# NSA layer of a four-layer hybrid trunk: queries projected ahead of the keys, compressed softmax in two halves, first scores ahead of the last projection

## The chip, the cores and the metric

One core of one Trainium2 chip. The metric is device time in microseconds (us) of one execution, lower is better; three runs give a median. The core has TensorE (PE, matrix products, with its weight loads shown apart as PEld), VectorE (DVE), ScalarE (ACT), GpSimd (POOL) and SyncE (SP, which here only starts DMA loads). Each engine works through its own queue in order, and semaphores tie the queues together.

## The reference, cut to what matters

A trunk of two layers on 256 tokens of width 1024. Each layer is FFN, token mixer, FFN, each wrapped in RMS norms with a residual. The first layer's mixer is native sparse attention (NSA), the second's is a softmax attention with a forget gate (FoX). Only the NSA mixer is touched:

```
q, kc, vc, ks, vs, kw, vw, gates = split(h @ w_in)       # 16 query heads of 64, 4 key groups
k_cmp = gelu(blocks(kc) @ w1[0] + b1[0]) @ w2[0]         # 15 blocks of 32 tokens, stride 16
v_cmp = gelu(blocks(vc) @ w1[1] + b1[1]) @ w2[1]
p_c   = masked_softmax(q @ k_cmp.T * scale + bias_c)     # compressed branch, 15 columns a head
o     = g0 * (p_c @ v_cmp) + g1 * attend(q, ks, vs) + g2 * attend(q, kw, vw)
return o @ w_out
```

With 256 tokens the selected branch sees all causal keys, as the window branch does, so both are full causal attentions.

## The kernel before, in words

Weights come in units of 1 MB (128 partitions by 2048 floats) in a ring of three slots. For each unit SP loads `raw`; ACT makes the rounded part `whi` (`hi`, L446), DVE the rest `wlo` (`lo`, L651), and PE multiplies in three products, which gives nearly fp32 precision. `hi` of unit u waits until PE is through with unit u - 3, so the splitting runs beside the products.

The NSA sub-layer has ten projection units, k = 0 to 9, of 256 columns each, then four units of output rows. PE takes the units in order; ACT copies each result from PSUM (`evacuate(k)`, L594, signal `proj_ready`). The column list in the SP queue sets the order: values of both branches (k = 0, 1), compressed keys and values (2, 3), selected keys (4), window keys (5), then the queries in four units (6 to 9), all 16 heads in eight pairs.

Between the projections the compressed branch is prepared. POOL shifts tokens by DMA (`pair_tokens`) into `pairs`; DVE gathers them and adds the position term into `flat` (`gather`, L818); PE runs `compress_hidden(kv)` (32 instructions), ACT copies (`part_out`, L598), PE folds (`compress_fold`), ACT takes GELU (L603), PE makes `compress_out(kv)`. Before, PE does hidden(0) behind k = 5, fold(0) behind 6, out(0) behind 7, hidden(1) behind 8, fold(1) behind 9. DVE's `gather(0)` stands in its queue behind `lo` of unit 7, two steps after the gate's reciprocal (L827). POOL also copies keys to the other half of the partitions by DMA (`kX`).

Then `attend` runs 16 stages n (head pair n // 2, branch n % 2) as a written-out order with a lag of three. In step i PE does `scores(i)`, something out of the table `after_scores`, `probs_T(i - 3)` (six transposes, L1186) and `heads(i - 4)`; DVE does `logits(i)` (L747), something out of `after_logits`, the copy of the transposes (L769) and `factors(i - 1)` (L756, L760); ACT does the exponentials of stage i (L542); POOL scales them (L372). PE's `probs_T(n)` waits for DVE's copy of stage n - 1. The compressed scores of all heads (32 products), their maximum, subtraction, exponential, sum and scaling (DVE L881 to L904, ACT L627), the values (L908) and eight transposes (L1282) with their two copies (L913) sit in steps 0, 1 and 2 of these tables, all behind the last projection.

Of the kernel before, what the change touches and what calls it, by code (L numbers as in the profile page):

```python
# [106 lines left out]
def trunk(nc, x, norm_g, w_gate, w_up, w_down, rel_bias, nsa_in, cmp_pe, cmp_w1, cmp_b1, cmp_w2,  # L107
          nsa_out, fox_in, fox_bf, fox_out, consts, onehots, out, scratch):
    with ExitStack() as ctx:
# [112 lines left out]
        kx_in = sem("kx_in")  # L222
# [43 lines left out]
        def _(sp):  # L266
# [33 lines left out]
            for s, kind in enumerate(KINDS):  # L300
# [17 lines left out]
                else:  # L318
                    w, wo = (nsa_in[0], nsa_out[0]) if kind == "nsa" else (fox_in[0], fox_out[0])
                    cols = [1792, 2304, 1024, 1280, 1536, 2048, 0, 256, 512, 768] if kind == "nsa" else [UC * k for k in (8, 9, 10, 11, 0, 1, 2, 3, 4, 5, 6, 7)]  # L320
# [13 lines left out]
        def _(pool):  # L334
# [72 lines left out]
            for r in range(2):  # L407
                pool.wait_ge(proj_ready, 5 + r)
                for a in range(2):
                    pool.dma_start(kX[64 * (1 - a):64 * (1 - a) + 64, r, :, :], kN[64 * a:64 * a + 64, r, :, :]).then_inc(kx_in, 16)  # L410
# [7 lines left out]
            nc.gpsimd.memset(pairs[:, :], 0.0).then_inc(probc_zero, 1)  # L418
            for n in range(H):
                scale_probs(n)  # L420
# [19 lines left out]
        def _(act):  # L440
# [91 lines left out]
            def attend(kind, out_unit):  # L532
# [16 lines left out]
                for i in range(N + LAG + 2):  # L549
                    if i >= LAG + 2 and (i - LAG - 1) % per == 0:  # L550
                        heads_hi((i - LAG - 1) // per - 1)
                    if i < N:
                        exps(n0 + i)
                    if i in (N, N + 2):
                        hi_static(out_unit + (i - N) // 2)
# [12 lines left out]
            for s, kind in enumerate(KINDS):  # L568
# [3 lines left out]
                else:  # L572
                    nproj = 10 if kind == "nsa" else 12

                    def evacuate(k):
# [4 lines left out]
                        if kind == "nsa":  # L580
                            if k >= 6:
                                dst, scale = qT[:, 2 * (k - 6):2 * (k - 6) + 2, :], DH ** -0.5
                            else:
                                dst = [vN[:, 0], vN[:, 1], kcv[:, 0], kcv[:, 1], kN[:, 0], kN[:, 1]][k]
# [14 lines left out]

                    def gelu(kv):  # L600
                        act.wait_ge(hid_mm, kv + 1)
                        for m in range(2):
                            last = nc.scalar.activation(hid[:, m, :], ps[:, MB, HID + m * 64:HID + m * 64 + G * NC], ACT.Gelu_apprx_tanh,  # L603
                                                        bias=smallT[:, 32 + 2 * kv + m:33 + 2 * kv + m])
                        last.then_inc(hid_ready, 1)
                    hi_static(u0 + 2)
                    for k in range(1, nproj):
                        evacuate(k - 1)
                        hi_static(u0 + k + 2)
# [3 lines left out]
                        if kind == "nsa" and k in (6, 9):  # L613
                            part_out((k - 6) // 3)
                        if kind == "nsa" and k == 7:
                            gelu(0)
                        if kind == "fox" and k == 3:
# [10 lines left out]
                    attend(kind, u0 + nproj + 2)  # L628
# [19 lines left out]
        def _(dve):  # L648
# [152 lines left out]
            for s, kind in enumerate(KINDS):  # L801
# [3 lines left out]
                else:  # L805
                    nproj = 10 if kind == "nsa" else 12

                    def gather(kv):
# [9 lines left out]
                        nc.vector.tensor_tensor(dst, src, pe_, ALU.add).then_inc(flat_ready, 1)  # L818
                    lo_static(u0 + 2)
                    for k in range(1, nproj):  # L820
                        lo_static(u0 + k + 2)
                        if kind == "nsa":
# [5 lines left out]
                            if k == 5:  # L828
# [4 lines left out]
                            if k == 8:  # L833
# [33 lines left out]
                    if kind == "nsa":  # L867
                        dve.wait_ge(hid_ready, 2)
                        dve.wait_ge(hidR_zero, 1)
                        for m in range(2):  # L870
                            src = hid[:, m, :]
                            src = bass.AP(src.tensor, src.offset, [list(src.ap[0]), [NC, G], [0, 4], [1, NC]])
                            last = nc.vector.tensor_copy(hidR[:, m, :, :, 0:NC], src)
                        last.then_inc(hidR_ready, 1)

                        dve.wait_ge(sc_mm, 1)
                        s3 = sc[:, :, :, :].rearrange("p t h c -> p (t h) c")

                        c1 = (P - CB) // CS + 1
                        s_ = ps[:, OB, 0:TT * H * NC].rearrange("p (t h c) -> p t h c", t=TT, c=NC)  # L880
                        nc.vector.tensor_tensor(sc[:, 0, :, 0:c1], s_[:, 0, :, 0:c1], bias[:, :, P + CB - 1:S:CS], ALU.add)  # L881
                        nc.vector.tensor_scalar(sc[:, 0, :, c1:NC], s_[:, 0, :, c1:NC], NEG, None, ALU.add)
                        nc.vector.tensor_tensor(sc[:, 1, :, :], s_[:, 1], bias[:, :, CB - 1:S:CS], ALU.add).then_inc(sc_step, 1)
                        dve.wait_ge(sc_step, 1)
                        nc.vector.tensor_reduce(cmx[:, :, :].rearrange("p t h -> p (t h)"), s3, AX.X, ALU.max).then_inc(sc_step, 1)
                        dve.wait_ge(sc_step, 2)
                        def spread(v):
                            return bass.AP(v[:, :, :].tensor, v[:, :, :].offset, [list(v[:, :, :].ap[0]), [1, TT * H], [0, NC]])
                        nc.vector.tensor_tensor(s3, s3, spread(cmx), ALU.subtract).then_inc(sc_logits, 1)

                    def compressed_probs():
                        dve.wait_ge(sc_exp, 1)
                        nc.vector.tensor_reduce(csum[:, :, :].rearrange("p t h -> p (t h)"), s3, AX.X, ALU.add).then_inc(sc_step, 1)
                        dve.wait_ge(sc_step, 3)
                        nc.vector.reciprocal(cfac[:, :, :], csum[:, :, :]).then_inc(sc_step, 1)
                        dve.wait_ge(sc_step, 4)

                        for t in range(TT):
                            last = nc.vector.scalar_tensor_tensor(cfac[:, t, :], cfac[:, t, :], cst[:, C_VALID + t:C_VALID + t + 1],
                                                                  gate[:, t, 0:H], ALU.mult, ALU.mult)  # L900
                        last.then_inc(sc_step, 1)
                        dve.wait_ge(sc_step, 5)
                        dve.wait_ge(probc_zero, 1)
                        nc.vector.tensor_tensor(probc.rearrange("p t h c -> p (t h) c")[:, :, 0:NC], s3, spread(cfac), ALU.mult).then_inc(probc_ready, 1)  # L904

                    def compressed_values():
                        dve.wait_ge(cmp_mm, 2)
                        nc.vector.tensor_copy(vcmp[:, :, :], ps[:, MB, 0:256].rearrange("p (g d) -> p g d", g=G)).then_inc(cmp_ready, 1)  # L908

                    def compressed_transposed():  # L910
                        for t in range(TT):
                            dve.wait_ge(probcT_mm, t + 1)
                            nc.vector.tensor_copy(probcT[:, :, t * P:(t + 1) * P],  # L913
                                                  ps[:, MB - t, :].rearrange("p (g n) -> p g n", g=G)).then_inc(probcT_ready, 1)
                    attend(kind, u0 + nproj + 2, {0: compressed_probs, 1: compressed_values, 2: compressed_transposed} if kind == "nsa" else {})
# [25 lines left out]
        def _(pe):  # L941
# [202 lines left out]
            def attend(kind, after_scores, out_rows, projected):  # L1144
# [22 lines left out]
                def scores(n):  # L1167
                    b = n % 2
                    if n >= 2:
# [9 lines left out]
                def probs_T(n):  # L1179
                    b = n % PB  # L1180
                    pe.wait_ge(prob_ready, n + 1)
                    if n >= 1:
                        pe.wait_ge(probT_ready, n)
                    for a in range(2):
# [4 lines left out]
                def heads(n):  # L1189
# [13 lines left out]
                    if compressed:  # L1203
                        if n == n0:
                            pe.wait_ge(probcT_ready, 2)
# [7 lines left out]
                for i in range(N + LAG + 1):  # L1213
# [10 lines left out]
                    if LAG <= i < N + LAG:  # L1224
                        probs_T(n0 + i - LAG)
# [6 lines left out]
            for s, kind in enumerate(KINDS):  # L1232
# [7 lines left out]
                for k in range(nproj):  # L1240
                    if k >= 2:
                        pe.wait_ge(proj_ready, pr0 + k - 1)
                        by_token = kind == "fox" and k < 4
                        (tokens if by_token else features)(u0 + k, (u0 + k) % RING, GB + k % 2)
                    if kind == "nsa" and k == 2:
                        gates(OB, 0, 48)
                    if kind == "nsa" and k == 5:
                        pe.wait_ge(gate_ready, 1)
                        for t in range(TT):
                            last = nc.tensor.transpose(ps[:, OB, S + 48 * t:S + 48 * (t + 1)], gateT[:, t * P:(t + 1) * P], cst[0:48, C_ID:C_ID + 48])  # L1250
# [69 lines left out]
```

## Time and the profile before

| what | value |
|---|---|
| median of 3 runs | 1083.14 us (1082.77 to 1083.49) |
| the profiled execution's own time | 1083.23 us |
| its span, first to last instruction | 1081.4 us |
| instructions | 18063 |
| PE busy | 1050.9 us, 97% of the span |
| DVE busy | 574.4 us, 53% |
| ACT busy | 483.0 us, 45% |
| mean granted PE clock | 0.993 of full |

The page gives busy times as shares of the span; a busy share is a mean over stretches with different limits. The NSA sub-layer lies between some 215 and 370 us of the span. Time of an execution stands 1.83 us over its span (launch and end).

### The profile page before, as it was taken

Reading aid. Unit: us, or ns where it says so; the run is one execution under the profiler, and the core shown is the slowest. Engines: PE = TensorE matmul, PEld = TensorE weight load, DVE = VectorE, ACT = ScalarE, POOL = GpSimd, SP = SyncE. Lnnn points to the kernel's source line nnn. Section 1 sums busy time; section 2 is a strip of 40 time slices with the busy share of each in tenths; the row PEclk is TensorE's granted clock in tenths of the full one; section 3 lists DMA queues with packets and bytes.
Section 4 is the critical chain, followed back from the end, with each engine's and each line's share of the span. In section 5 each row is a group of like instructions: output and inputs, shape, how many; then the busy total and the mean of one; then the engine's idle time right before and its main releaser. Section 6 shows DMA issues by size and latency. Waiting matters only on the chain.

```text
span 1081.4 us, 18063 instructions
## 1 busy us (share of the span) xinstructions
PE 1050.9 (97%) x7489; PEld 962.5 (89%) x7489; DVE 574.4 (53%) x645; ACT 483.0 (45%) x615; POOL 104.5 (10%) x207
## 2 busy tenths in 40 slices
PE   6999999999989999999999999999999999999997
PEld 6897999999856799999989999999999779999996
DVE  4543454554487555444566445445555765454444
ACT  4434434454375354444354434444456635434432
POOL 0100000122054200000011000000123420000000
PEclk8999999999989999999999999999999999999999
DMA  9686555477401275655646565555555136556551
GB/s 278 213 304 224 167 192 194 156 221 248 135 2 40 82 244 180 194 187 166 197 150 225 171 196 187 194 183 167 196 156 194 41 97 226 168 190 194 172 178 39
DMA packets 137813, 187.80 MB, mean 174 GB/s; under 512 B 7249, under 2 KB 120102, under 8 KB 137766
## 3 DMA queue, kind: packets, MB, share of 16 engines
q1 hardware_dynamic: 133702, 172.90, 49.8%
q0 software_dynamic: 3920, 14.18, 3.8%
q8 instruction: 34, 0.56, 0.2%
q14 instruction: 13, 0.11, 0.0%
q10 hardware_dynamic: 144, 0.07, 0.0%
HBM read 184.48 MB, written 1.07 MB: 172 GB/s over the span
## 4 chain that ended last, share of the span: by engine, by line
PE 89%; DVE 4%; ACT 2%; issue 2%; POOL 2%; SPq 1%; DMA 1%; DVEq 0%; ACTq 0%
PE ps L943 86%; PE ps L1186 2%; DVE normed L683 1%; POOL ms_half L343 1%; DVE normed L663 1%; ACT ps L466 1%; DMA raw<-in_ffn_w_gate 1%; ACT whi L446 1%; POOL rstd L349 1%; PE ps L1023 1%; DVE xlo L691 0%; DVE probT_buf L769 0%; DVE res L672 0%; SPq L291 0%; SPq L282 0%
## 5 line engine op out<-in xcount | busy, mean ns | idle before, releaser
L651 DVE TENSOR_TENSOR wlo<-raw,whi 128x2048 fp32r<-128x2048 f32 x156 | 358.0, 2295 | 320.1 <-ACT whi L446 320.1
L943 PE MATMUL ps<-xhi,whi 128*128 128x256 f32 x1536 | 435.8, 284 | 0.0
L943 PE MATMUL ps<-xlo,whi 128*128 128x256 f32 x1536 | 434.6, 283 | 0.0
L943 PE MATMUL ps<-xhi,wlo 128*128 128x256 f32 x1536 | 434.6, 283 | 0.0
L446 ACT ACTIVATE whi<-raw 128x2048 fp32r<-128x2048 f32 x156 | 297.5, 1907 | 112.7 <-PE ps L943 110.7
L943 PEld LDWEIGHTS ps<-xhi,whi 128*128 128x128 f32 x1536 | 294.6, 192 | 3.4 <-issue 2.0
L943 PEld LDWEIGHTS ps<-xlo,whi 128*128 128x128 f32 x1536 | 294.7, 192 | 1.6 <-issue 0.2
L943 PEld LDWEIGHTS ps<-xhi,wlo 128*128 128x128 f32 x1536 | 294.7, 192 | 0.0
L943 PE MATMUL ps<-whi,hhi 128*128 128x512 f32 x320 | 125.0, 391 | 0.0
L943 PE MATMUL ps<-wlo,hhi 128*128 128x512 f32 x320 | 125.0, 391 | 0.0
L943 PE MATMUL ps<-whi,hlo 128*128 128x512 f32 x320 | 124.5, 389 | 0.0
L943 PE MATMUL ps<-whi,xhi 128*128 128x256 f32 (+1 forms) x320 | 104.5, 326 | 8.7 <-DVE xlo L691 8.7
L943 PE MATMUL ps<-wlo,xhi 128*128 128x256 f32 (+1 forms) x320 | 101.8, 318 | 0.0
L943 PE MATMUL ps<-whi,xlo 128*128 128x256 f32 (+1 forms) x320 | 101.7, 318 | 0.0
L493 ACT ACTIVATE hhi<-work 128x512 fp32r<-128x512 f32 x36 | 22.7, 631 | 164.3 <-DVE work L698 164.3
L943 PEld LDWEIGHTS ps<-whi,xhi 128*128 128x128 f32 x320 | 62.0, 194 | 14.9 <-issue 7.9
L347 POOL TENSOR_SCALAR ms<-ss 128x1 f32<-128x1 f32 x14 | 4.8, 341 | 718.3 <-ACT ps L470 718.3
L943 PEld LDWEIGHTS ps<-whi,hlo 128*128 128x128 f32 x320 | 60.1, 188 | 12.8
L943 PEld LDWEIGHTS ps<-whi,hhi 128*128 128x128 f32 x320 | 60.2, 188 | 11.5
L943 PEld LDWEIGHTS ps<-wlo,hhi 128*128 128x128 f32 x320 | 60.2, 188 | 11.0
L484 ACT ACTIVATE work<-ps 128x512 f32<-128x512 f32 x44 | 26.3, 598 | 91.6 <-PE ps L943 91.5
L943 PEld LDWEIGHTS ps<-whi,xlo 128*128 128x128 f32 x320 | 62.0, 194 | 3.9
(171 smaller groups left out, 832.0 us busy)
## 6 DMA issues: line engine op xcount, KB each, us to landing
raw<-in_ffn_w_gate SPq DMA_DIRECT2D x44, 1024.0 KB, 5.3
raw<-in_ffn_w_up SPq DMA_DIRECT2D x44, 1024.0 KB, 5.3
raw<-in_ffn_w_down SPq DMA_DIRECT2D x44, 1024.0 KB, 4.9
raw<-in_fox_w_in SPq DMA_DIRECT2D x12, 1024.0 KB, 5.4
raw<-in_nsa_w_in SPq DMA_DIRECT2D x10, 1024.0 KB, 5.3
big<-in_nsa_cmp_w POOLq DMA_DIRECT2D x2, 2048.0 KB, 11.3
raw<-in_nsa_w_out SPq DMA_DIRECT2D x4, 1024.0 KB, 5.0
raw<-in_fox_w_out SPq DMA_DIRECT2D x4, 1024.0 KB, 4.9
```

Of the source, the lines that this page charges most:

```text
L343: nc.gpsimd.tensor_scalar(ms_half[:, j:j + 1], ss_half[:, j:j + 1], scale / D, eps, ALU.mult, ALU.add).then_inc(half_mean, 1)
L349: nc.gpsimd.tensor_tensor(rstd[:, i:i + 1], ms[:, i:i + 1], half[:, :], ALU.pow).then_inc(rstd_ready, 1)
L446: nc.scalar.activation(whi[:, slot, :], raw[:, slot, :], ACT.Copy).then_inc(w_hi, 1)
L466: nc.scalar.activation(ps[:, OB, :], res[:, t, 0:512], ACT.Square, accum_out=ss_half[:, j:j + 1]).then_inc(half_sumsq, 1)
L484: nc.scalar.activation(silu_sb, ps[:, GB, :], ACT.Silu).then_inc(silu_ready, 1)
L493: nc.scalar.activation(dst[:, 0:2, :], src.rearrange("p (a n) -> p a n", a=2), ACT.Copy).then_inc(hhi_ready, 1)
L651: nc.vector.tensor_tensor(wlo[:, slot, :], raw[:, slot, :], whi[:, slot, :].bitcast(F32), ALU.subtract).then_inc(w_lo, 1)
L663: nc.vector.tensor_tensor(normed[:, t, :].rearrange("p (a n) -> p a n", a=2), ps[:, YB + 2 * t:YB + 2 * t + 2, :], g_post[:, :].rearrange( ...
L683: nc.vector.scalar_tensor_tensor(normed[:, t, cols], res[:, t, cols], rstd[:, i:i + 1], g_pre[:, cols], ALU.mult, ALU.mult).then_inc(norme ...
L943: return nc.tensor.matmul(out_, l, r, start=start, stop=stop)
L1023: last = nc.tensor.transpose(ps[:, GB + 2 * t + b, k * P:(k + 1) * P], normed[:, t, (4 * b + k) * P:(4 * b + k + 1) * P], ident)
L1186: last = nc.tensor.transpose(ps[:, GB + a, k * P:(k + 1) * P], prob[b][:, a, k * P:(k + 1) * P], ident)
```

## The change

- The projection order: the first two query units move ahead of the selected and window keys (columns 0 and 256 become k = 4 and 5, the keys k = 6 and 7).
- PE: `compress_hidden(0)` behind k = 4 and not 5, fold(0) behind 5, out(0) behind 6; `compressed_scores(0)`, for the first eight heads, and hidden(1) behind 7; fold(1) behind 8. `scores(0)` and `scores(1)` come ahead of projection 9, which is now in `attend` behind `scores(1)`. The second half of the compressed scores and out(1) follow `scores(2)`. The transposes are split in four (step 3), two (ahead of `probs_T(4)`) and two (ahead of `probs_T(5)`).
- DVE: `gather(0)` directly behind the gate's reciprocal (k = 4), `gather(1)` at 6, the keys' copy at 7, first softmax half at 8 and 9; in `attend` the second half: logits in step 2, maximum in 3, probabilities in 5; transposed copies in 3, 7 and 8; `lo` of unit 11 in step 1.
- ACT: exponential of the first half at k = 8, second GELU at 9, projection 9's copy behind the exponentials of stage 1, the second half's exponential behind those of stage 4.
- POOL: the `kX` copies go behind both `pair_tokens`, the load of the second `w1` and the clearing of `pairs`, with a semaphore for each branch.

```diff
-cols = [1792, 2304, 1024, 1280, 1536, 2048, 0, 256, 512, 768]
+cols = [1792, 2304, 1024, 1280, 0, 256, 1536, 2048, 512, 768]
@@ POOL: moved behind the memset of pairs
-for r in range(2):
-    pool.wait_ge(proj_ready, 5 + r)
+for r in range(2):
+    pool.wait_ge(proj_ready, 7 + r)
@@ ACT
+if kind == "nsa" and k == 9: gelu(1)          # behind evacuate(8)
+if k in (5, 8): part_out((k - 5) // 3)
+if k == 6: gelu(0)
+if k == 8: compressed_exp(0)
-    evacuate(nproj - 1)
-    gelu(1)
-    act.wait_ge(sc_logits, 1)
-    nc.scalar.activation(sc[:, :, :, :], sc[:, :, :, :], ACT.Exp).then_inc(sc_exp, 1)
+    attend(kind, u0 + nproj + 2, {1: lambda: evacuate(9), 4: lambda: compressed_exp(1)})
@@ DVE
-if k == 5:
+if k == 4:
     gather(0)
-if k == 7:
+if k == 6:
     gather(1)
+if k == 8:
+    compressed_logits(0)
+    compressed_max(0)
+if k == 9:
+    compressed_probs(0)
-attend(..., {0: compressed_probs, 1: compressed_values, 2: compressed_transposed})
+attend(..., {0: spread_hidden, 1: lambda: lo_static(u0 + 11), 2: second_compressed, 3: first_transposed,
+             5: lambda: compressed_probs(1), 7: lambda: later_transposed(2), 8: lambda: later_transposed(3)})
+def second_compressed():
+    compressed_logits(1)
+    dve.wait_ge(cmp_mm, 2)
+    nc.vector.tensor_copy(vcmp[:, :, :], ps[:, MB, 0:256]...).then_inc(cmp_ready, 1)
+def first_transposed():
+    compressed_max(1)
+    dve.wait_ge(probcT_mm, 1)
+    nc.vector.tensor_copy(probcT[:, 0:2, :], ps[:, MB, :]...).then_inc(probcT_ready, 1)
@@ PE
+for k in range(9):
+    if k >= 2: project(k)
+    if k == 4: compress_hidden(0)
+    if k == 5: (gate transposes); compress_fold(0)
+    if k == 6: compress_out(0)
+    if k == 7:
+        pe.wait_ge(gate_ready, 2)
+        pe.wait_ge(cmp_ready, 1)
+        compressed_scores(0)
+        compress_hidden(1)
+    if k == 8: compress_fold(1)
+attend(kind, {1: last_projection, 2: second_compressed, 3: first_T}, {7: lambda: later_T(2), 8: lambda: later_T(3)},
+       out_rows, (proj_ready, pr0 + nproj))
+def second_compressed():
+    pe.wait_ge(sc_step, 1)
+    pe.wait_ge(proj_ready, pr0 + 10)
+    compressed_scores(1)
+    compress_out(1)
+def first_T():
+    pe.wait_ge(probc_ready, 1)
+    pe.wait_ge(cmp_ready, 2)
+    # four transposes for groups 0 and 1
```

## Rows read from the trace of the kernel before

**Rows 1.** The page, busy time, share of the span and instructions of each engine.
```profile
PE 1050.9 (97%) x7489; PEld 962.5 (89%) x7489; DVE 574.4 (53%) x645; ACT 483.0 (45%) x615; POOL 104.5 (10%) x207
```
**Rows 2.** Waits of PE, 230 to 420 us: total, times, longest.
```profile
PE ps L1282 <- DVE vcmp L908: 2.7, 1, 2.7
...
PE ps L943 <- DVE xlo L691: 1.2, 1, 1.2
PE ps L943 <- DVE nmax L747: 0.8, 1, 0.8
...
PE ps L943 <- DVE flat L818: 0.5, 1, 0.5
```
**Rows 3.** Stretches of 4 us: engines' busy time, then clock, DMA share, GB/s.
```profile
core 0: us, PE busy (x) PEld busy (x) DVE busy (x) ACT busy (x) POOL busy (x), PEclk, DMA share, GB/s
...
296.00:300.00 4.00, 1.39 (x13) 0.85 (x11) 3.90 (x21) 2.47 (x9) 0.00 (x0) 0.83 0.00 0
300.00:304.00 4.00, 3.14 (x16) 2.50 (x16) 3.62 (x19) 3.58 (x16) 1.73 (x5) 0.50 0.02 4
304.00:308.00 4.00, 3.71 (x26) 2.50 (x24) 3.40 (x18) 1.89 (x9) 2.44 (x7) 0.82 0.01 2
...
372.00:376.00 4.00, 2.83 (x24) 2.62 (x23) 4.00 (x6) 2.19 (x6) 0.79 (x2) 1.00 0.00 0
```
**Rows 4.** PE in order of time: start, duration, what, idle before.
```profile
257.19 3.67 PE L943 MATMUL ps<-big,flat 128*64 128x256 f32 x32 [0.54 <-DVE flat L818]
...
289.92 3.76 PE L943 MATMUL ps<-kcmp,qT 128*128 128x30 f32 x32
...
300.86 1.94 PE L1282 MATMUL ps<-cst,pairs 128*128 128x128 f32 x8 [2.67 <-DVE vcmp L908]
...
306.87 0.85 PE L1186 MATMUL ps<-cst,work 128*128 128x128 f32 x6 [0.29 <-DVE probT_buf L769]
```
**Rows 5.** DVE in order of time, around the first gather.
```profile
247.35 2.29 DVE L651 TENSOR_TENSOR wlo<-raw,whi 128x2048 fp32r<-128x2048 f32 x1 [6.22 <-ACT whi L446]
...
249.88 1.75 DVE L827 RECIPROCAL work<-work 48x256 f32<-48x256 f32 x1
...
255.32 1.81 DVE L818 TENSOR_TENSOR flat<-pairs,smallT 128x960 f32<-128x960 f32 x1
```
**Rows 6.** ACT in order of time.
```profile
250.68 0.60 ACT L594 ACTIVATE kN<-ps 128x512 f32<-128x512 f32 x1 [3.37 <-PE ps L943]
251.17 1.90 ACT L446 ACTIVATE whi<-raw 128x2048 fp32r<-128x2048 f32 x1
256.44 0.60 ACT L594 ACTIVATE kN<-ps 128x512 f32<-128x512 f32 x1 [3.36 <-PE ps L943]
...
289.27 0.51 ACT L603 ACTIVATE hid<-ps,smallT 128x60 f32<-128x60 f32 x2
289.80 1.28 ACT L627 ACT_TABLE_LOAD   x1
...
297.24 0.40 ACT L542 ACTIVATE work<-work,nmax 128x128 f32<-128x128 f32 x1 [0.51 <-DVE nmax L747]
...
298.92 0.18 ACT L542 ACTIVATION_READ_ACCUMULATOR work<-work,nmax 128x1 f32 x1
```
**Rows 7.** DVE in order of time, in the opening of the attention.
```profile
296.02 0.28 DVE L747 CUSTOM_DVE_ANT_0 work<-ps,bias 128x128 f32<-128x128 f32 x1
...
297.13 0.65 DVE L893 TENSOR_REDUCE csum<-sc 128x32 f32<-128x480 f32 x1
...
298.61 0.66 DVE L904 TENSOR_TENSOR pairs<-sc,cfac 128x480 f32<-128x480 f32 x1
...
302.02 1.50 DVE L913 COPY flat<-ps 128x512 f32<-128x512 f32 x2
...
305.76 0.96 DVE L769 COPY probT_buf<-ps 128x768 f32<-128x768 f32 x1
```
**Rows 8.** The chain that ended last, two pieces in the steady attention.
```profile
310.75 1.66 PE ps L943 x16
312.41 0.81 PE ps L1186 x6
```

More of the change, by code:

```diff
@@ L418, in _ @@
             nc.gpsimd.memset(pairs[:, :], 0.0).then_inc(probc_zero, 1)
+            for r in range(2):
+                pool.wait_ge(proj_ready, 7 + r)
+                for a in range(2):
+                    pool.dma_start(kX[64 * (1 - a):64 * (1 - a) + 64, r, :, :], kN[64 * a:64 * a + 64, r, :, :]).then_inc(kx_in[r], 16)
             for n in range(H):
@@ L530, in ffn, with attend @@
                 hi_static(u0 + 33)
-            def attend(kind, out_unit):
+            def attend(kind, out_unit, after_exps):
                 n0, p0, N = STAGE0[kind], PAIR0[kind], STAGES[kind]
@@ L598, in part_out, with compressed_exp @@
                         nc.scalar.activation(hid_part, ps[:, MB, 0:HID], ACT.Copy).then_inc(part_ready, 1)
+                    def compressed_exp(r):
+                        act.wait_ge(sc_logits, r + 1)
+                        v = sc[:, :, 8 * r:8 * r + 8, :]
+                        nc.scalar.activation(v, v, ACT.Exp).then_inc(sc_exp, 1)
                     def gelu(kv):
@@ L608, in _ @@
                         evacuate(k - 1)
+                        if kind == "nsa" and k == 9:
+                            gelu(1)
                         hi_static(u0 + k + 2)
@@ L622, in _ @@
                             nc.scalar.activation(fT[:, 3, :], fT[:, 2, :], ACT.Ln, bias=1.0).then_inc(f_ln, 1)
-                    evacuate(nproj - 1)
                     if kind == "nsa":
-                        gelu(1)
-                        act.wait_ge(sc_logits, 1)
-                        nc.scalar.activation(sc[:, :, :, :], sc[:, :, :, :], ACT.Exp).then_inc(sc_exp, 1)
-                    attend(kind, u0 + nproj + 2)
+                        attend(kind, u0 + nproj + 2, {1: lambda: evacuate(9), 4: lambda: compressed_exp(1)})
+                    else:
+                        evacuate(nproj - 1)
+                        attend(kind, u0 + nproj + 2, {})
                     for k in range(2, 3):
@@ L818, in gather, with heads_part, spread, compressed_logits @@
                         nc.vector.tensor_tensor(dst, src, pe_, ALU.add).then_inc(flat_ready, 1)
+                    def heads_part(v, r):
+                        return v[:, :, 8 * r:8 * r + 8]
+                    def spread(v, r):
+                        v = heads_part(v, r)
+                        return bass.AP(v.tensor, v.offset, [list(d) for d in v.ap] + [[0, NC]])
+                    c1 = (P - CB) // CS + 1
+                    def compressed_logits(r):
+                        dve.wait_ge(sc_mm, r + 1)
+                        hs = slice(8 * r, 8 * r + 8)
+                        s_ = ps[:, OB, 0:TT * H * NC].rearrange("p (t h c) -> p t h c", t=TT, c=NC)
+                        nc.vector.tensor_tensor(sc[:, 0, hs, 0:c1], s_[:, 0, hs, 0:c1], bias[:, hs, P + CB - 1:S:CS], ALU.add)
+                        nc.vector.tensor_scalar(sc[:, 0, hs, c1:NC], s_[:, 0, hs, c1:NC], NEG, None, ALU.add)
+                        nc.vector.tensor_tensor(sc[:, 1, hs, :], s_[:, 1, hs, :], bias[:, hs, CB - 1:S:CS], ALU.add).then_inc(sc_step, 1)
@@ new lines, in compressed_max, with compressed_probs @@
+                    def compressed_max(r):
+                        s_ = heads_part(sc, r)
+                        dve.wait_ge(sc_step, 5 * r + 1)
+                        nc.vector.tensor_reduce(heads_part(cmx, r), s_, AX.X, ALU.max).then_inc(sc_step, 1)
+                        dve.wait_ge(sc_step, 5 * r + 2)
+                        nc.vector.tensor_tensor(s_, s_, spread(cmx, r), ALU.subtract).then_inc(sc_logits, 1)
+                    def compressed_probs(r):
+                        s_ = heads_part(sc, r)
+                        hs = slice(8 * r, 8 * r + 8)
+                        dve.wait_ge(sc_exp, r + 1)
+                        nc.vector.tensor_reduce(heads_part(csum, r), s_, AX.X, ALU.add).then_inc(sc_step, 1)
+                        dve.wait_ge(sc_step, 5 * r + 3)
+                        nc.vector.reciprocal(heads_part(cfac, r), heads_part(csum, r)).then_inc(sc_step, 1)
+                        dve.wait_ge(sc_step, 5 * r + 4)
+                        for t in range(TT):
+                            last = nc.vector.scalar_tensor_tensor(cfac[:, t, hs], cfac[:, t, hs], cst[:, C_VALID + t:C_VALID + t + 1],
+                                                                  gate[:, t, hs], ALU.mult, ALU.mult)
+                        last.then_inc(sc_step, 1)
+                        dve.wait_ge(sc_step, 5 * r + 5)
+                        dve.wait_ge(probc_zero, 1)
+                        nc.vector.tensor_tensor(heads_part(probc, r)[:, :, :, 0:NC], s_, spread(cfac, r), ALU.mult).then_inc(probc_ready, 1)
@@ new lines, in spread_hidden @@
+                    def spread_hidden():
+                        dve.wait_ge(hid_ready, 2)
+                        dve.wait_ge(hidR_zero, 1)
+                        for m in range(2):
+                            src = hid[:, m, :]
+                            src = bass.AP(src.tensor, src.offset, [list(src.ap[0]), [NC, G], [0, 4], [1, NC]])
+                            last = nc.vector.tensor_copy(hidR[:, m, :, :, 0:NC], src)
+                        last.then_inc(hidR_ready, 1)
+                    def second_compressed():
+                        compressed_logits(1)
+                        dve.wait_ge(cmp_mm, 2)
+                        nc.vector.tensor_copy(vcmp[:, :, :], ps[:, MB, 0:256].rearrange("p (g d) -> p g d", g=G)).then_inc(cmp_ready, 1)
@@ L867, in _ @@
                     if kind == "nsa":
[L868 to L876, printed above, removed]
@@ L891, in compressed_probs @@
[L891 to L904, printed above, removed]
@@ L906, in compressed_values @@
[L906 to L914, printed above, removed]
@@ L1142, in compress_out, with attend @@
                 last.then_inc(cmp_mm, 1)
-            def attend(kind, after_scores, out_rows, projected):
+            def attend(kind, after_scores, before_heads, out_rows, projected):
                 n0, p0, N = STAGE0[kind], PAIR0[kind], STAGES[kind]
@@ L1168, in scores @@
                     b = n % 2
+                    if kind == "nsa" and n < 2:
+                        pe.wait_ge(kx_in[n], 32)
                     if n >= 2:
@@ L1177, in scores, with probs_T @@
                     last.then_inc(scores_mm, 1)
-                def probs_T(n):
+                def probs_T(n, extra=None):
                     b = n % PB
@@ L1204, in heads @@
                         if n == n0:
-                            pe.wait_ge(probcT_ready, 2)
+                            pe.wait_ge(probcT_ready, 1)
+                            pe.wait_ge(sc_step, 6)
+                        elif n in (8, 12):
+                            pe.wait_ge(probcT_ready, n // 4)
                         for a in range(2):
@@ L1224, in attend @@
                     if LAG <= i < N + LAG:
-                        probs_T(n0 + i - LAG)
+                        probs_T(n0 + i - LAG, before_heads.get(i))
                     if i == N + LAG:
@@ L1239, in _ @@
                 nproj = 10 if kind == "nsa" else 12
[L1240 to L1250, printed above, removed]
-                        last.then_inc(gateT_mm, 1)
-                    if kind == "nsa" and k in (5, 8):
-                        compress_hidden((k - 5) // 3)
-                    if kind == "nsa" and k in (6, 9):
-                        compress_fold((k - 6) // 3)
-                    if kind == "nsa" and k == 7:
-                        compress_out(0)
-                    if kind == "fox" and k == 1:
-                        gates(MB, 48, GWC)
-                    if kind == "fox" and k == 5:
-                        pe.wait_ge(cum_ready, 1)
-                        mm(ps[:, MB, 0:S], cst[0:2 * H, C_SEL:C_SEL + P], cum[:, :], True, True).then_inc(cum_mm, 1)
@@ L1289, in heads_of, with project @@
+                def project(k):
+                    pe.wait_ge(proj_ready, pr0 + k - 1)
+                    by_token = kind == "fox" and k < 4
+                    (tokens if by_token else features)(u0 + k, (u0 + k) % RING, GB + k % 2)
                 def heads_of(k):
```

123 lines of the change are left out of this document (74 added, 49 removed).

## The prediction, made before the changed kernel ran

> **What bounds the kernel now.** I read the page first: PE is busy for 97% of the span [rows 1]. So a reordering pays only where PE stands still or runs at the lower clock, and costs wherever it makes PE stand. Next the waits of PE around the NSA sub-layer [rows 2]: 0.5 us for `flat`, 0.8 for the logits (L747), 2.7 for the compressed branch behind `vcmp`; PE's own order of time adds 0.3 before the second `probs_T` [rows 4]. Together 4.3 us. Then the granted clock [rows 3]: 0.83, 0.50 and 0.82 in three stretches of 4 us. With 0.5 as the low level (1.2 of 2.4 GHz), 1.36 us of the first and 1.44 of the last were low, so the clock fell at about 298.6 and rose at about 305.4. PE had been idle 0.80 us and then, after the short scores, was in an idle of 2.67. It worked from 300.86 [rows 4] to 305.4 at half clock, 4.6 us, which lost 2.3. What this opening costs in all is 4.3 + 2.3 = 6.6 us, and that is also the most that the change can give back here: every product is still done, and steady attention shows PE without a wait (the chain stays on PE there [rows 8]).
>
> **The change part by part.** I walk the new order with the old durations. Up to the end of projection 4, which is where `evacuate(4)` starts, 250.68 [rows 6], nothing is moved.
>
> *Wait A, the first gather.* `compress_hidden(0)` now stands directly behind projection 4 and needs `gather(0)`. The gather is one of DVE's items of step 4: `lo` of unit 6 starts at 247.35 because it waits for ACT, then comes the reciprocal from 249.88 for 1.75, to 251.63, then the gather, 1.81 [rows 5]. It ends at 253.4. PE is done at 250.6 and stands 2.8 us, with everything behind it in its queue. Before, a projection of 5.76 us (the distance of two `evacuate` starts [rows 6]) and the gate's transposes lay between, and 0.54 was left [rows 4]. The gather needs nothing later than the paired tokens, whose DMAs are long issued, so nothing but DVE's own queue sets this. `lo` of unit 7 is then behind the gather by about 0.4 us and is not wanted for another ten.
>
> *Projections 5 to 8.* With PE 2.3 us later than before, I checked each wait. The second `w1` is loaded behind hidden(0) and is wanted 20 us later. `pairs` is cleared and `kX` copied some 10 us ahead of `scores(0)`, though POOL's copies now wait behind both token shifts, the `w1` load and the clearing. The first softmax half on DVE and ACT (about 2.5 us with its table load of 1.28 [rows 6]) lies under projection 8. The `kcmp` copy ends about 1 us before PE asks; this is the thinnest cover, and what it misses comes straight to PE. SP's load of unit 14 waits for `lo` of unit 11, now in `attend`: some 10 us later, but wanted after all 16 stages. Cost nothing.
>
> *Wait B, the last evacuation.* After projection 8 PE has the fold (0.5), `scores(0)` and `scores(1)`, projection 9 (5.76) and `scores(2)`. A stage's scores take half of 1.66 [rows 8], 0.83. That makes 8.8. ACT in the same time has, in order, `evacuate(8)` 0.6, a table load 1.28, GELU 0.5, `hi` of unit 11 1.9, the table load back 1.28, the exponentials of stages 0 and 1, 1.87 each (297.24 to 299.10), and `evacuate(9)` 0.6 [rows 6]: 9.9. PE's second compressed scores wait for that copy: 9.9 - 8.8 = 1.1; I take 1.05 as some ACT instructions overlap by 0.1.
>
> *Wait C, step 4.* `probs_T(1)` waits for DVE's copy of stage 0. From the end of `scores(3)` DVE has `logits(3)` 1.11 (296.02 to 297.13 [rows 7]), the half maximum and subtraction, the copy of 512 columns 0.75 (half of 1.50) and the copy of stage 0, 0.95 [rows 7]. Half of a 480-column operation lies between half of 0.65 and all of it; half the columns suggest half plus the overhead of a small one, 0.37, so 0.74 for two. Sum 3.6. PE meanwhile does four transposes (0.55, as eight took 1.94 at half clock [rows 4]), `probs_T(0)` 0.81 [rows 8] and `scores(4)` 0.83: 2.2. PE stands 1.4.
>
> *Wait D, step 6.* The second half's probabilities sit ahead of the copy of stage 2. The whole took from 297.13 to 299.27, 2.1 [rows 7]; the half lies between 1.05 and 2.1, I take 1.4. DVE: 1.11 + 1.4 + 0.95 = 3.5; PE: `probs_T(2)` 0.81 and heads with scores 1.66 [rows 8]: 2.5. PE stands 1.0. After that DVE has the two late copies, some 0.4 each, and the next waits come out with 0.2 to 0.4 us to spare.
>
> The halving itself adds no product; the compressed scores are 16 + 16 for 32 [rows 4]. *Sum at full clock:* A 2.8 + B 1.05 + C 1.4 + D 1.0 = 6.3 against 6.6 removed: -0.3 us. The bounds: C and D each from 0.4 less to 0.9 more by the two ends for a half, B from 0 to 1.3; so from -2.1 to +1.8.
>
> *The clock.* The trace has no idle of 2.8 us inside dense projections, so its price is unknown: nothing at the least, and at the most 3.4, half of the 6.8 us that the low stretch lasted, if all of it were work. The nearest row is the fall at 298.6: it came in an idle of 2.67 us with 0.80 shortly before. An idle of 1.17 to 1.2 with dense work around it [rows 2] left the clock at 1.00 [rows 3]. A is far nearer the first. I take a fall, at the 2.3 us that the old one lost. Waits B and C come with light work between them, the 16 products of 30 columns among it, as in the old opening; a second fall there is a little likelier than not. It also costs 2.3 us, but DVE goes on at its pace, and about half of C and D (1.2) closes up: 1.1 net.
>
> The Trainium skill (TensorE: Matmul & The Clock Gate, "Why this matters for your kernels") says that the clock holds if no idle between bursts of matmuls passes about 3 us. The row of this trace speaks against it, for a gap of 2.67, but with 0.80 shortly before. By that rule wait A would leave the clock alone, and the sum would stay at -0.3; by the row it is 2.3 higher.
>
> **Total.** -0.3 + 2.3 + 1.1 = +3.1 us on the profiled 1083.23 gives 1086.3; the median of the runs stands 0.1 under that execution, so 1086.2.
>
> **The rivals.** 0.2% (2.2 us) is what a measurement of this kernel can tell from no change.
> - *One fall only* (after A, or in the opening): -0.3 + 2.3 = +2.0, 1085.1. For it: B and C are each shorter than the old idle. 28 in 100.
> - *The clock holds through all four waits*: -0.3, 1082.8. This is the skill's rule, as a mechanism: idles of at most 2.8 cost themselves alone. Against it stands the fall at 298.6 [rows 3]. 10 in 100.
> - *Faster: DVE keeps up in the opening*, so that B, C and D do not come, and the clock holds. Then -6.6 + 2.8 = -3.8, 1079.3. It decides when DVE's 3.6 us behind `scores(3)` come under PE's 2.2, and likewise in step 6; against it stand the durations [rows 7]. With a fall after A it would be -1.5, no measurable change. 8 in 100.
> - *Worse:* the falls last over more work, or C and D stay beside them: -0.3 + 3.4 + 2.3 = +5.4 at the end, 1088.5; middle 1087.8. 12 in 100.
> - *My forecast*, two falls: 42 in 100.
>
> **How the numbers follow.** Slower by over 2.2: nearly all of the forecast (0.38), nearly half of the one-fall case (0.13), all of the worse (0.12): 0.63. Faster: the faster rival and a touch of the bounds: 0.09. Within: the rest, 0.28. The range for 8 in 10 leaves out the faster rival and the far end of the worse: 1082.6 to 1088.3. For the forecast alone it is 1085.0 to 1087.4.
>
> **What would show it.** In the profile after: a wait of PE for `flat` of 2.8 us near 250.6, followed by stretches of clock under 1.00 in projection 5; the wait before L1282's old place gone; a wait for ACT's `qT` copy of about 1 us behind `scores(2)`; waits for `probT_buf` of 1.4 and 1.0; a second low stretch there; two table loads more on ACT; from stage 8 on the old pace. The prediction is wrong if the clock row shows 1.00 after `flat`, if the opening's waits are missing, or if a cover I counted as free (the `kcmp` copy, the `kX` copies) shows as a wait of PE.

## The result, and the profile after

The changed kernel takes 1086.24 us (median of 7 runs, 1084.33 to 1087.67) against 1083.06 us (7 runs, 1082.77 to 1083.49): 3.2 us more, ratio 1.0027 with a 95% interval of 1.0016 to 1.0038. It is slower by 0.27%, and a ratio of 1 lies outside the interval. The profiled execution took 1085.29 us with a span of 1083.5 us, 2.1 us over that of the kernel before; the median span over the seven executions is 1084.2 us. An execution's time stands between 1.8 and 3.3 us over its span in these seven, not always by the 1.83 us of the profile before.

The waits of PE around the NSA sub-layer, against [rows 2] (same columns):

```profile
PE ps L1229 <- DVE probT_buf L780: 3.0, 4, 1.2
PE ps L982 <- DVE flat L829: 2.6, 1, 2.6
PE ps L982 <- DVE xlo L702: 1.2, 1, 1.2
PE ps L982 <- ACT qT L597: 1.1, 1, 1.1
```

Of the kernel before, one line of the same view belongs beside these:

```profile
PE ps L1186 <- DVE probT_buf L769: 1.3, 3, 0.7
```

The waits for `vcmp` (2.7) and for the logits (0.8) are gone. In their place stand the gather (2.6, before 0.5), the copy of projection 9 (1.1, new), and the copies of the transposes (3.0 in four waits, before 1.3 in three). In PE's order of time, against [rows 4]:

```profile
252.92 5.36 PE L982 MATMUL ps<-big,flat 128*64 128x256 f32 x32 [2.65 <-DVE flat L829]
...
298.12 1.94 PE L982 MATMUL ps<-kcmp,qT 128*128 128x30 f32 x16 [1.12 <-ACT qT L597]
307.18 0.84 PE L1229 MATMUL ps<-cst,work 128*128 128x128 f32 x6 [0.79 <-DVE probT_buf L780]
313.97 0.85 PE L1229 MATMUL ps<-cst,normed 128*128 128x128 f32 x6 [1.24 <-DVE probT_buf L780]
```

These are waits A, B, C and D: 2.65, 1.12, 0.79 and 1.24, together 5.8 us where 4.3 stood before. The 32 instructions of `compress_hidden(0)` also took 5.36 us where they took 3.67. Stretches of 4 us show why, against [rows 3]:

```profile
core 0: us, PE busy (x) PEld busy (x) DVE busy (x) ACT busy (x) POOL busy (x), PEclk, DMA share, GB/s
252.00:256.00 4.00, 3.08 (x20) 1.88 (x22) 3.06 (x2) 0.71 (x1) 2.33 (x4) 0.73 0.78 230
256.00:260.00 4.00, 4.00 (x31) 2.92 (x28) 0.00 (x0) 0.38 (x1) 1.41 (x2) 0.84 0.94 277
296.00:300.00 4.00, 2.88 (x27) 2.43 (x26) 1.36 (x9) 3.69 (x17) 1.63 (x4) 1.00 0.82 261
300.00:304.00 4.00, 4.00 (x28) 3.23 (x28) 1.70 (x9) 0.15 (x2) 1.18 (x4) 0.70 0.00 0
304.00:308.00 4.00, 3.21 (x25) 2.51 (x23) 3.93 (x17) 1.86 (x8) 1.03 (x3) 0.87 0.01 2
```

The clock is below 1.00 twice: behind wait A, 2.16 + 1.28 = 3.4 us, and behind wait B, 2.4 + 1.04 = 3.4 us, at 1.2 of 2.4 GHz. PE had work through nearly all of both, so they lose 1.7 us each. The sum: waits 5.8 - 4.3 = +1.5, clock 3.4 - 2.3 = +1.1, together +2.6. The spans differ by 2.1. Most of the rest lies ahead of the sub-layer: `evacuate(4)` starts at 250.31 against 250.68 before, 0.4 us earlier. From there to the last head product of the NSA attention, which ends at 360.19 against 358.16, the change costs 2.4 us. What follows it takes 723.3 us in both traces, and in all the others below.

DVE's order of time shows wait A's cause as it was walked from [rows 5]:

```profile
246.99 2.29 DVE L662 TENSOR_TENSOR wlo<-raw,whi 128x2048 fp32r<-128x2048 f32 x1 [6.22 <-ACT whi L446]
249.19 0.28 DVE L903 TENSOR_SCALAR work<-work 48x256 f32<-48x256 f32 x1
249.51 1.75 DVE L905 RECIPROCAL work<-work 48x256 f32<-48x256 f32 x1
251.18 1.69 DVE L829 TENSOR_TENSOR flat<-pairs,smallT 128x960 f32<-128x960 f32 x1
```

The row to see is the first: DVE was idle for 6.22 us ahead of it. The gather stands behind the reciprocal by its place in the queue and not for want of time.

### The profile page after: what moved, and what is told of

Read it like the earlier page. It is cut to its first block, busy times and chain, and to the rows that moved or that the text cites. A ratio compares the mean times of both kernels' runs of the same rounds, so it can differ in the third digit from the quotient of the medians.

```text
span 1083.5 us, 18080 instructions
## 1 busy us (share of the span) xinstructions
PE 1051.4 (97%) x7489; PEld 962.7 (89%) x7489; DVE 575.7 (53%) x656; ACT 485.6 (45%) x618; POOL 104.5 (10%) x207
## 4 chain that ended last, share of the span: by engine, by line
PE 88%; DVE 4%; ACT 3%; issue 2%; POOL 1%; SPq 1%; DMA 1%; DVEq 0%; ACTq 0%
PE ps L982 86%; PE ps L1229 1%; DVE normed L694 1%; POOL ms_half L343 1%; ACT whi L446 1%; DVE normed L674 1%; ACT ps L466 1%; POOL rstd L349 1%; DVE probT_buf L780 1%; DMA raw<-in_ffn_w_gate 1%; PE ps L1062 1%; DVE xlo L702 0%; DVE res L683 0%; ACT work L542 0%; SPq L291 0%
```

## The experiments

Each ran against the kernel before on the same chip, whose medians were 1083.13 us beside the runs of experiments 1, 3, 4 and the 18 products of 2; 1083.73 beside the 12 products, experiment 5 and the three reorderings of 6; and 1083.50 beside the last kernel of 6 and the first run of 7. Where two kernels of different sessions are compared, it is by their ratios, and such a difference is uncertain by some 1.5 us (the two intervals taken together).

**1. The gather ahead of the gate's work.**

```diff
 if k == 4:
+    gather(0)
     dve.wait_ge(gate_exp, 1)
     ... tensor_scalar, reciprocal
-if k == 4:
-    gather(0)
 def part_out(kv):
+    act.wait_ge(gate_ready, 1)
```

> The changed kernel with one swap on DVE: the first gather ahead of the gate's add and reciprocal (ACT's part_out then waits for the reciprocal, which was ordered before by the queue). My theory: wait A goes from 2.65 us to about 0.7 (it loses 0.28 + 1.75 of DVE work ahead of it), no fall of the clock follows, so 1.9 + 1.7 = 3.6 us less than the changed kernel, about 1082.6, with the opening as it was. Rival 1, the clock after A costs nothing of its own (or the fall comes all the same): 1.9 us less, 1084.3. Rival 2, the excess lies not in A but outside the span: no change, 1086.

1082.90 us (12 runs), ratio 0.9996, interval 0.9988 to 1.0005: no difference from the kernel before, and 3.3 us under the changed one. The median span fell from 1084.2 to 1080.85. Wait A was 0.8 us:

```profile
PE ps L983 <- DVE flat L830: 0.8, 1, 0.8
```

The clock stood at 1.00 in both stretches from 252 to 260. So without wait A and its fall the excess of the change is gone. Rival 2 falls. Rival 1's 1.9 us is at the edge of what the intervals leave; experiment 2 shows the cost of the clock by itself.

The opening did not stay as it was, though. In this trace, whose time (1084.65 us) is the second longest of the 12, the clock fell at about 296.1 and was low for 10.2 us, where it had been low for 3.4:

```profile
296.00:300.00 4.00, 4.00 (x22) 4.00 (x21) 0.64 (x3) 1.10 (x6) 0.00 (x0) 0.52 0.06 20
300.00:304.00 4.00, 4.00 (x20) 3.23 (x20) 1.88 (x12) 0.00 (x0) 1.62 (x4) 0.50 0.00 0
```

So the verdict on this experiment rests on the times of its 12 executions and not on the span of its trace.

**2. Products in wait A, 18 and then 12.**

```diff
 if k == 4:
+    for _ in range(18):                      # 12 in the second kernel
+        mm(ps[:, MB, 0:P], ident, ident, True, True)
     compress_hidden(0)
```

> The changed kernel with 18 extra 128x128 products of the identity (their result is overwritten) ahead of compress_hidden(0), so that PE works through most of wait A. They take about 18 x 0.135 = 2.4 us, under the 2.65 of the wait, so the length of the wait with them is the same and only the clock is touched. My theory: clock stays at 1.00 after A, 1.7 us less than the changed kernel, 1084.5. Rival, the low clock after A is hidden by other engines' waits: no change, 1086.2.

1086.54 us (10 runs), ratio 1.0031 (1.0021 to 1.0040): nothing gained. The size of the products was my error: such a product took 0.22 us, not the 0.135 of a transpose, so the 18 filled 3.95 us and PE began `compress_hidden(0)` 1.3 us later than without them. Behind them the clock was held, and the stretch from there to the compressed scores shrank:

```profile
254.25 0.44 PE L982 MATMUL ps<-big,flat 128*64 128x256 f32 x2
...
276.53 1.64 PE L982 MATMUL ps<-kcmp,qT 128*128 128x30 f32 x14
```

That is 22.28 us; in the changed kernel it runs from 252.92 to 276.88, 23.96 us. The fall behind wait A costs 1.68 us. This trace gave the gain back in the opening: its low stretch there lasted 6.8 us against 3.4 in the changed kernel. With 12:

> The changed kernel with 12 extra products in wait A in place of 18. The 18 took 3.95 us (0.22 each) and so made the wait 1.3 us longer than it was, while the stretch behind it up to the compressed scores shrank from 23.96 to 22.28 us, by 1.68. Twelve take 2.6 us, as long as the wait of 2.65. My theory: 1.7 us less than the changed kernel, 1084.5. Rival, what the clock gives back at A is lost again in the opening, where a longer fall follows: no change, 1086.2.

1084.87 us (11 runs), ratio 1.0013 (1.0004 to 1.0022), 1.5 us less than the changed kernel by the ratios (0.0014 of 1083), which is no more than its uncertainty. The median span fell by only 1.1, from 1084.2 to 1083.1. The sign of my theory is likely, its size is not shown, and the rival, a longer fall in the opening, is open for the executions without a trace. The trace is of the fastest of the 11 executions (1082.87 us, span 1081.0), and brought something else: waits of 1.12 (ACT's `qT` copy), 1.52 and 1.24 us in the opening, and

```profile
300.00:304.00 4.00, 3.21 (x29) 1.00 0.01 2
304.00:308.00 4.00, 3.27 (x28) 1.00 0.00 0
```

the clock at 1.00 throughout (columns: stretch, its length and PE's busy time, clock, DMA share, GB/s). The second fall is not certain for this order, and without it wait C is 1.52 and not 0.79: at the low clock PE comes later to a copy that DVE makes at its own pace. From the first compressed scores (275.26) to the end of the last head product (357.70) it took 82.44 us; the changed kernel took 83.31 (276.88 to 360.19). So its fall in the opening cost 0.9 us net of what wait C gave back.

**3. Wait A alone, in the kernel before.**

```diff
-if k == 5:
+if k == 4:
     gather(0)
-if kind == "nsa" and k in (5, 8):
-    compress_hidden((k - 5) // 3)
+if kind == "nsa" and k in (4, 8):
+    compress_hidden((k - 4) // 4)
-if kind == "nsa" and k in (6, 9):
-    part_out((k - 6) // 3)
+if kind == "nsa" and k in (5, 9):
+    part_out((k - 5) // 4)
```

> The kernel before with one part of the change alone: the first gather on DVE and compress_hidden(0) on PE one projection earlier, the copy behind it too. My theory: wait A of 2.65 us appears in place of 0.54 and the clock falls for 3.4 us: 2.1 + 1.7 = 3.8 us over before, 1086.9. Rival, the clock does not fall here: 2.1 over, 1085.2. Rival, nothing (the time comes back in the opening, whose compressed work starts earlier): 1083.1.

1087.00 us (5 runs), ratio 1.0034 (1.0021 to 1.0047): 3.7 us over, with a wait of 2.7 for `flat` and the clock at 0.70 and 0.87 behind it. This part by itself makes the slowdown, and all else in the change about pays for itself. The trace places it: the compressed scores start at 293.65 against 289.92, 3.7 us later, and from there to the end of the attention it takes 68.0 us against 68.2. It shows one more thing. The clock fell again at about 298.0, and PE had not waited since wait A:

```profile
296.00:300.00 4.00, 4.00 (x29) 3.50 (x29) 2.48 (x8) 0.13 (x1) 0.00 (x0) 0.75 0.00 0
```

**4. The copy of projection 9 ahead of the exponentials of stage 1.**

```diff
-attend(kind, u0 + nproj + 2, {1: lambda: evacuate(9), 4: lambda: compressed_exp(1)})
+attend(kind, u0 + nproj + 2, {0: lambda: evacuate(9), 4: lambda: compressed_exp(1)})
```

> The changed kernel with the copy of projection 9 on ACT behind the exponentials of stage 0 and not of stage 1. My theory: wait B (1.12 us) goes, and with it the second fall of the clock (1.7 us); but DVE then is behind by more and waits C and D grow by up to 1.3 in all: 1.5 us less than the changed kernel, 1084.7. Rival, waits C and D alone make the fall: it stays, and only 1.1 less or nothing is gained.

1083.46 us (11 runs), ratio 1.0001 (0.9993 to 1.0010), 2.8 less than the changed kernel where I expected 1.5. Wait B is gone, and C and D did not grow (0.69 and 1.24). Its trace has the same wait A, yet no fall:

```profile
PE ps L982 <- DVE flat L829: 2.7, 1, 2.7
```
```profile
252.00:256.00 4.00, 2.83 (x26) 1.00 0.75 229
```

The second fall, which my theory took away with wait B, is still there. It begins at about 299.15 and lasts 3.4 us, and PE had not waited since 253.16:

```profile
296.00:300.00 4.00, 4.00 (x36) 3.92 (x37) 2.09 (x12) 2.86 (x14) 0.48 (x2) 0.89 0.48 169
```

So the 2.7 us by which this trace's span is under that of the changed kernel divide in two. 1.4 us are gained ahead of the compressed scores (275.46 against 276.88), where the clock did not fall. 1.25 us are gained behind them (82.06 us against 83.31), about wait B alone, as the rival has it. How much of the 2.8 us of the medians comes from executions without a fall can't be told from one trace. In the traces of three other kernels with this wait (the changed one, experiment 3, experiment 5) the clock fell.

**5. The copies of the transposes ahead of the compressed softmax.**

```diff
+late = kind == "nsa" and i in (3, 5)
-if i in after_logits:
+if i in after_logits and not late:
     after_logits[i]()
 if LAG <= i < N + LAG:
     probs_T(n0 + i - LAG)
+if late:
+    after_logits[i]()
```

> The changed kernel with one reordering on DVE: in steps 3 and 5 of the attention the copy of the transposed probabilities goes ahead of the compressed work (maximum with its copy in step 3, probabilities in step 5). My theory: wait D (1.24 us) goes; wait C (0.79) shrinks, since probs_T(1) no longer waits and only heads(0), 0.8 us later in PE's queue, still needs the compressed transposes; waits A and B and both falls stay. About 1.9 us less than the changed kernel, 1084.3. Rival, DVE is simply full there and the wait moves to the next stage (stage 4 or 6): less than 0.5 gained, 1086.

1085.77 us (11 runs), ratio 1.0016 (1.0007 to 1.0025), by the ratios 1.2 less than the changed kernel, which is within its uncertainty. The waits of 0.79 and 1.24 are gone. What is late next is POOL's scaling: DVE makes the factors of stage 4 as long after that stage's logits as before (2.3 us, behind the probabilities in both orders), and PE now gets there sooner:

```profile
PE ps L1331 <- POOL work L372: 0.5, 1, 0.5
```

Between theory and rival: the wait of 1.24 moved, but to some 0.5. The trace is of the longest of the 11 executions, and its low stretch in the opening lasted 6.8 us in place of 3.4, so its span (1084.5) shows nothing of the gain.

**6. All three reorderings, and the gather one step earlier still.**

> The changed kernel with the three reorderings together: gather ahead of the gate's reciprocal, copy of projection 9 ahead of the exponentials of stage 1, copies of the transposes ahead of the compressed softmax. My theory: the gains add up, as each removes another wait: of the span 3.35 us (gather) and 2.7 (evacuation) as measured, and 1.9 for the copies, so 8 us less than the changed kernel at most, and 1 to 2 us less than that where two of them remove the same fall of the clock: 1079.5. That beats both kernels. Rival, DVE bounds the opening whatever the order: the second and third add nothing to the first, 1082.5.

1079.32 us (5 runs), ratio 0.9962 (0.9948 to 0.9976), 4.4 us faster than the kernel before. By the ratios that is 7.0 us under the changed kernel, where the three gave 3.4, 2.8 and 1.2 by themselves: the gains add up. PE's waits:

```profile
PE ps L1233 <- DVE probT_buf L781: 1.3, 3, 0.7
PE ps L986 <- DVE xlo L703: 1.2, 1, 1.2
PE ps L986 <- DVE flat L833: 0.8, 1, 0.8
PE ps L1332 <- POOL work L372: 0.5, 1, 0.5
PE ps L986 <- issue: 0.5, 1, 0.5
```

The clock was 1.00 over the whole of 200 to 1000 us. Then, with all three:

```diff
+if k == 3:
+    gather(0)
 if k == 4:
-    gather(0)
     dve.wait_ge(gate_exp, 1)
```

> All three reorderings, with the first gather moved one step further ahead on DVE, behind the low half of unit 5, where DVE waits some 6 us for ACT anyway. The paired tokens land about 243.6 us, the gather ends at 245.5 and delays nothing. My theory: what is left of wait A (0.79 us) goes, the rest stays as in the run with all three: 0.8 us less than that, span 1076.2, about 1078.5. Rival, the paired tokens land later than I read, and the low half of unit 6 is late: no gain or a loss, 1079.3 or more.

1078.29 us (5 runs), ratio 0.9957 (0.9943 to 0.9970), 5.2 us faster than the kernel before. That it is faster than the kernel ahead of it is not clear of the intervals, but the wait for `flat` is gone. The gather sits in DVE's old idle time and delays nothing:

```profile
238.99 2.29 DVE L663 TENSOR_TENSOR wlo<-raw,whi 128x2048 fp32r<-128x2048 f32 x1 [3.47 <-ACT whi L446]
244.06 1.86 DVE L833 TENSOR_TENSOR flat<-pairs,smallT 128x960 f32<-128x960 f32 x1 [2.78 <-DMA pairs<-work]
247.50 2.29 DVE L663 TENSOR_TENSOR wlo<-raw,whi 128x2048 fp32r<-128x2048 f32 x1 [1.58 <-ACT whi L446]
```

**7. Products in the old opening's wait.**

```diff
 def compressed_T():
+    for _ in range(12):
+        mm(ps[:, GB, 0:P], ident, ident, True, True)
     pe.wait_ge(probc_ready, 1)
```

> The kernel before with 12 extra 128x128 products of the identity ahead of its compressed transposes, where PE waited 2.67 us (their result is overwritten). They take 12 x 0.213 = 2.6 us. My theory: the clock does not fall there, or falls for less, which gives back the most of the 2.3 us that I put down to it: 1081 us, span 1079. The change thus gave the waits of the old opening and its fall against its own. Rival, the old fall comes from the 0.80 us wait and the light products before it as much as from the 2.67: it stays, and nothing is gained, 1083.

1085.22 us (11 runs), ratio 1.0015 (1.0006 to 1.0024): slower, against my theory. Yet the profiled execution took 1081.91 us with a span of 1080.1 and the clock at 1.00 in all of the opening. One kernel, two outcomes, so I took two more traces of it.

> The kernel before with 12 products in its wait, once more for a second trace: its profiled execution held the clock and had a span of 1080.1, while most other executions had spans of 1083 to 1085. My explanation: in those the clock falls already on the 0.80 us wait and the light products ahead, and the 12 extra products then take about 5.1 us in place of 2.6, longer than the wait that they fill; the span is then 1083 to 1085 and the trace shows clock 0.50 under them. Rival: the clock holds there too and the time goes elsewhere.

> The same kernel a third time, for the same reason: if its span is above 1082, the trace should show the extra products at 0.50 and lasting about 5 us; if it is about 1080, the clock at 1.00 through them.

The first had a span of 1080.2 us: the 24 instructions of the 12 products from 297.96 in 2.94 us, clock 1.00. The second had 1083.8 us:

```profile
289.13 0.37 PE L943 MATMUL ps<-kN,qT 64*128 64x128 f32 x1
...
289.99 3.76 PE L943 MATMUL ps<-kcmp,qT 128*128 128x30 f32 x32
293.68 0.58 PE L943 MATMUL ps<-kN,qT 64*128 64x128 f32 x1
...
300.45 4.57 PE L943 MATMUL ps<-cst 128*128 128x128 f32 x24
```
```profile
288.00:292.00 4.00, 4.00 (x37) 3.60 (x37) 0.48 (x2) 2.28 (x4) 0.00 (x0) 1.00 0.10 35
292.00:296.00 4.00, 4.00 (x28) 3.31 (x27) 2.15 (x5) 0.00 (x0) 0.00 (x0) 0.70 0.00 0
296.00:300.00 4.00, 4.00 (x22) 3.67 (x21) 3.90 (x19) 2.47 (x9) 0.00 (x0) 0.50 0.00 0
300.00:304.00 4.00, 4.00 (x21) 3.56 (x18) 2.14 (x15) 3.52 (x16) 1.64 (x4) 0.52 0.01 4
```

Low for 2.4 us of the second stretch, the clock fell at about 293.6; one instruction of the scores, 0.37 us at 289.13, takes 0.58 at 293.68. PE had not stood still: busy 4.00 of 4.00, and no wait since the one of 0.53 at 257.25. What it had just done was the 32 products of 30 columns. So my explanation held in its second half (the extra products took 4.57 us with the clock low) and was wrong in its first: no wait was needed for the fall. The traces of experiments 3 and 4 showed the same, each behind such light products. That these products bring it on is likely and not shown, since the clock stayed at 1.00 behind the same row in the other two traces of this kernel.

## Why the prediction was right, point by point

- *Forecast and total.* 1086.2 predicted, 1086.24 measured, slower as forecast. Agreement to 0.04 us is luck: the changed kernel's own executions spread over 3.3 us. For the profiled execution the sum gave 1086.3 and it took 1085.29, so +3.1 was measured as +2.1; and the median, put 0.1 us under that execution, stands 0.95 over it. The two misses cancel. What holds is the structure, two falls and four waits.
- *Wait A.* 2.8 predicted, 2.65 found. Experiments 1 and 3 show it to be the cause, from both sides: without it the excess goes, and alone it makes it. The excess of 3.2 us is what is left of larger costs and gains, so taking away another cost, as experiment 4 did, nearly closes it too.
- *Its fall.* Taken at 2.3 us by the nearest row, measured at 1.68 (experiment 2). The row was dear because the low stretch of before lasted 6.8 us and this one 3.4. That the clock falls at all I took as settled for the forecast; one trace of four with this wait shows 1.00 behind it. The case with one fall was therefore well worth its chance.
- *Wait B.* 1.05 predicted, 1.12 found. Experiment 4 took it away and gained 2.8 us in the medians, against 1.05 + 1.1 in my terms. In its trace the stretch behind the compressed scores gained 1.25 us, the wait alone, with the second fall still there.
- *Waits C and D.* 1.4 and 1.0 predicted, 0.79 and 1.24 found, or 1.52 and 1.24 where the clock holds (experiment 2). The half of a 480-column operation took 0.40 where I took 0.37, and the half's probabilities 1.44 us for 1.4. The bounds that I gave for wait C were too wide for their reason: by the two ends for a half it goes from 0.1 less to 0.6 more, and 0.79 lies under that because PE was late at the low clock.
- *The second fall.* 1.1 net predicted, from 2.3 less 1.2. Found: 1.7 gross less the 0.7 by which wait C closed, 1.0, or 0.9 by the stretches of experiment 2. The forecast laid it to waits B and C with light work between. That step is not borne out: it came without wait B in experiment 4 and without any wait in experiments 3 and 7, and stayed away with waits of 1.12, 1.52 and 1.24 in the trace with 12 products. What decides it is open.
- *Old opening.* I put 6.6 us on it. The waits of 4.3 are the rows' own. The 2.3 of the clock is right for that execution as a gross figure. Where the clock held (experiment 7), the next wait on DVE's copy grew from 0.29 to 1.1, so the net cost of that fall was nearer 1.5; from the compressed scores to the end of the attention it took 68.2 us with the fall and 67.1 without. My sum did not net it, as it did the new one.
- *Steps at no cost.* The `kcmp` copy, `kX` on POOL, the load behind unit 11: none shows as a wait of PE. ACT makes five table loads around the sub-layer where it made three, as forecast.
- *The skill's rule.* The Trainium skill (TensorE: Matmul & The Clock Gate, "Why this matters for your kernels") holds the clock safe below some 3 us of idle. The traces here speak against it as a safe line: eight of the thirteen have a fall in this sub-layer, and no idle of PE there is over 2.67 us. The same page ("What's actually happening") says that what the chip looks at runs free of the kernel's start; that agrees with the same wait of 2.65 giving 1.00 in one execution and 0.70 to 0.73 in three.

## What to carry to other kernels

When a consumer moves ahead in one queue, its producer must move ahead in the other queue past everything that it does not need; look for the idle time of the producer's engine ahead of its present place, as DVE's 6.22 us here. Order inside a step is a choice: the copy that another engine waits for goes first, the work for later stages behind it. With those orders put right the same change turns from 0.27% slower to 0.43% faster. A change near zero is a small difference of larger costs and gains, and each of them can be worked on by itself. And where a kernel's executions differ by whether the clock fell, take more than one trace before a clock term is believed.

## What the runs showed of the hardware

- Falls of the granted clock in the opening differ between executions of one kernel: none in two traces of experiment 7, one beginning near 293.6 us in the third. Behind the wait of 2.65 us there was none in one trace of four.
- In three traces (experiments 3, 4 and 7) the clock fell with PE never idle for 36 us and more by the profile, each time during or within 2 us of light products: 30 columns, 32 in 3.76 us, or 16 in 1.97 us with 16 small ones behind them. The clock held behind the same row in other traces.
- Low stretches of 3.4, 6.8 and 10.2 us in the opening cost 0.9, 2.3 and 3.3 us, a third of their length or less, where PE at the full clock would have waited for DVE and ACT for part of the time. From the first compressed scores to the end of the attention, in four traces with the same order there (the falls begin at different places):

| trace | clock low in the opening | this stretch |
|---|---|---|
| 12 products (experiment 2) | 0 us | 82.4 us |
| changed kernel | 3.4 us | 83.3 us |
| 18 products (experiment 2) | 6.8 us | 84.7 us |
| gather ahead of the gate (experiment 1) | 10.2 us | 85.7 us |

- Filling a wait with dummy products is no safe cure. A 128x128 product of fp32 took 0.22 us at the full clock; twelve of them took 2.94 us at the full clock and 4.57 where the clock was low, longer than the wait of 2.67 that they were to fill.
